# Late sums one at a time in the projection, and GpSimd as the starter of half the block writes

## The reference

```python
shift, scale, gate = jnp.split(jax.nn.silu(c) @ w_ada[layer] + b_ada[layer], 3, axis=-1)
h = rmsnorm(x, norm_g[layer]) * (1.0 + scale[:, None]) + shift[:, None]
u = h @ w_in[layer]
# ... gated delta heads and RWKV heads from u ...
x = x + gate[:, None] * (jnp.concatenate([ya, yb], axis=-1) @ w_out[layer])
```

## Time and profile before

| | |
|---|---|
| profiled execution | 3534.95 us, span 3533.2 us |
| granted TensorE clock, mean | 0.924 |
| projection | 0 to about 1468 us; TensorE busy 1191.83, VectorE 834.79 |
| product L2018, one per pair period | first at 309.4, last at 876.2 us: 81.0 us apart |
| recurrence, 1468 to 2070 | TensorE busy 504.81, VectorE 301.16, ScalarE 136.51, GpSimd 0.13 |
| L2049, sums of 128 x 512 | 240, 180.4 us busy; 239.4 us of standing ahead of them |
| L1365, starts of reads by GpSimd | 256, 137.5 us |

### The profile page before, as it was taken

How to read it: one execution, slowest core, us unless ns; L and a number is a source line. 1 busy time by engine, 2 the same in 40 slices (tenths; PEclk the granted TensorE clock), 3 DMA queues, 4 the chain that set the end, 5 groups by cost and what they waited for, 6 DMA issues and landing times. The chain is left out here.

```text
span 3533.2 us, 71437 instructions
## 1 busy us (share of the span) xinstructions
PE 2973.7 (84%) x30614; PEld 2473.7 (70%) x30614; DVE 2012.3 (57%) x3463; ACT 1012.2 (29%) x1636; POOL 708.9 (20%) x526
## 2 busy tenths in 40 slices
PE   5898888878788888388998967886979999998897
PEld 2586777666667777388888856775867877786484
DVE  5556556565554565345555556774241799997123
ACT  3243334333232222112222223322012444323102
POOL 0001111110010111000000000002864334374283
PEclk9899999988888998699999979997999999999998
DMA  9525555545555556323333224433423222221322
GB/s 388 199 76 156 154 171 166 163 152 162 171 179 175 189 180 202 118 81 94 96 86 101 74 83 145 130 115 152 155 84 125 79 83 78 84 84 60 119 95 72
DMA packets 265242, 465.90 MB, mean 132 GB/s; under 512 B 108224, under 2 KB 156576, under 8 KB 258544
## 3 DMA queue, kind: packets, MB, share of 16 engines
q1 hardware_dynamic: 213152, 364.52, 31.4%
q0 software_dynamic: 20672, 67.27, 6.5%
q10 hardware_dynamic: 31120, 29.72, 2.7%
HBM read 382.40 MB, written 81.63 MB: 131 GB/s over the span
## 5 line engine op out<-in xcount | busy, mean ns | idle before, releaser
L1365 POOL DMA_DIRECT2D arena_p<-in_w_ada x256 | 137.5, 537 | 1208.2 <-DVE arena_p L2049 624.3
L1139 PE MATMUL pjl<-high,w_high 128*128 128x512 f32 x816 | 325.4, 399 | 29.0 <-DVE low L2810 16.4
L1140 PE MATMUL pjl<-low,w_high 128*128 128x512 f32 x816 | 320.8, 393 | 0.0
L1141 PE MATMUL pjl<-high,w_low 128*128 128x512 f32 x816 | 320.6, 393 | 0.0
L2049 DVE SCALAR_TENSOR_TENSOR arena_p<-arena_p,csk 128x512 f32<-128x512 f32 x240 | 180.4, 752 | 239.4 <-DMA arena_p<-in_w_ada 235.0
L3238 DVE SCALAR_TENSOR_TENSOR arena<-arena,par 128x512 f32<-128x512 f32 x232 | 293.1, 1263 | 6.8
L1122 POOL TENSOR_TENSOR w_low<-ring_o,w_high 128x1024 fp32r<-128x1024 f32 x88 | 226.7, 2576 | 6.9
L1249 PE MATMUL xu<-h_high,wh_in 128*128 128x512 f32 x512 | 221.0, 432 | 0.0
L2880 POOL TENSOR_TENSOR w_low<-ring_o,w_high 128x1024 fp32r<-128x1024 f32 x64 | 169.3, 2646 | 250.1 <-ACT w_high L3067 249.7
L1120 POOL TENSOR_TENSOR w_high<-ring_o,cst 128x1024 fp32r<-128x1024 f32 x88 | 171.1, 1944 | 213.0 <-PE pjl L1141 67.8
L1268 DVE TENSOR_TENSOR wl_in<-ring,wh_in 128x1024 fp32r<-128x1024 f32 x136 | 165.9, 1220 | 82.8 <-ACT wh_in L1261 82.5
(11 more groups left out here) (506 smaller groups left out, 6922.4 us busy)
## 6 DMA issues: line engine op xcount, KB each, us to landing
ring<-in_w_lr SPq DMA_DIRECT2D x136, 512.0 KB, 4.5
arena_p<-in_w_ada POOLq DMA_DIRECT2D x256, 256.0 KB, 3.5
arena_p<-in_w_ada SPq DMA_DIRECT2D x32, 1024.0 KB, 8.8
ring_o<-in_w_out SPq DMA_DIRECT2D x64, 512.0 KB, 3.8
ring_o<-in_w SPq DMA_DIRECT2D x64, 512.0 KB, 3.8
arena_r<-rk_d SPq DMA_DIRECT2D x47, 384.0 KB, 4.7
rk_d<-arena_p SPq DMA_DIRECT2D x72, 192.0 KB, 2.0
arena_p<-gate_rows SPq DMA_DIRECT2D x32, 386.0 KB, 6.5
```

The costliest lines, as they stand in the source:

```text
L1139: pe.matmul(lat, wh[:, c], ah, start=kk == 0, stop=False)
L1140: pe.matmul(lat, wh[:, c], al, start=False, stop=False)
L1141: last = pe.matmul(lat, wl[:, c], ah, start=False, stop=kk == KT - 1)
L1365: pool.dma_start(late[:, x % 2], io["w_ada"][8 + x // 16, :, x % 16]).then_inc(S[f"p_la{x % 2}"], 16)
```

## The change

1. `later(n)` becomes `later(due)`: one call does at most one sum, and none once `due` sums are done. The calls are spread over the lines between VectorE's other work, also inside `sums` and `streams`.
2. The 16 sums leave the front and stand beside the LoRA mixes, the gate chain and the first mixes; their four column products move to the start of period 0, into the columns `pair_cols`, and TensorE waits there for `late_kept(0)` (p_ld) before the LoRA products.
3. GpSimd's first 16 reads are cut in two, 11 and 5, with the first two pairs of gate rows between.
4. Three sums of every period but the first are done in the tail of the one before.
5. In the recurrence GpSimd starts the four block writes that ScalarE started, on a semaphore of their own (r_g1); SyncE waits for both.

```diff
@@ front_vector, columns
             parts(2)
-            later(6)
             weights(6)
             row(6)
-            later(6)
             weights(7)
             row(7)
-            later(4)
             mods(3)
@@ gpsimd, projection
-            late_reads(pool, 0, 16)
-            front_pool(pool)
+            late_reads(pool, 0, 11)
+            front_pool(pool, lambda: late_reads(pool, 11, 16))
             late_reads(pool, 16, 256)
@@ tensor, period
+                if i == 0:
+                    pe.wait_ge(S["p_ld"], 1)
                 lora_products(0)
@@ tensor
             columns()
-            late_columns(pe, front_cols, 16)
...
             pe.wait_ge(S["b_gc"], 6)
+            late_columns(pe, pair_cols, 16)
@@ vector, sums and streams
                     link(dve.tensor_tensor_scan(...))
+                later(16 * i + 32)
                 dve.tensor_tensor(sg, cs, sg, ALU.subtract).then_inc(S["p_cs"], 1)
...
                 link(dve.tensor_tensor(bb, kk, av, ALU.mult))
+                later(16 * i + 32)
...
                 dve.tensor_tensor(bb, bb, gn, ALU.mult)
+                later(16 * i + 32)
                 dve.tensor_tensor(kd, kd, gn, ALU.mult)
+                later(16 * i + 32)
                 dve.tensor_tensor(sg, kk, sg, ALU.mult)
@@ vector, head
                 if more:
                     weights(m + 2)
-                    later(3)
+                    later(due)
                     weights(m + 3)
-                    later(3)
+                    later(due)
                 dve.wait_ge(S["q_nl"], 48 * (h + 1))
                 link(dve.tensor_tensor(qkv[:, 1], qkv[:, 1], sqk, ALU.mult))
+                later(due)
                 dve.scalar_tensor_tensor(qkv[:, 0, 0:LAT], ...)
+                later(due)
                 for d in range(2):
                     link(dve.tensor_tensor(KB[:, d], KB[:, d], qkv[:, 1], ALU.mult))
+                    later(due)
                 for d in range(2):
                     dve.tensor_tensor(KBG[:, d], KB[:, d], EG[:, d], ALU.mult)
+                    later(due)
@@ vector, period
                 link(dve.scalar_tensor_tensor(kk, k, prm(i, R_KK), nr, ALU.mult, ALU.mult))
+                later(due)
                 sums(i, 0)
-                later(2)
+                later(due)
                 weights(m + 2)
-                later(1)
+                later(due)
                 weights(m + 3)
-                later(2)
+                later(due)
                 streams(i, 0)
-                later(1)
+                later(due)
...
                 sums(i, 1)
-                later(3)
+                later(due)
                 weights(m + 6)
-                later(3)
+                later(due)
                 streams(i, 1)
+                while x_[0] < due:
+                    later(due)
...
                 if i < PAIRS - 1:
+                    later(due + 1)
                     mixes(i + 1, 2, "p_mv")
+                    later(due + 2)
                     weights(m + 9)
+                    later(due + 3)
@@ vector, later
-            def later(n):
-                for x in range(x_[0], min(x_[0] + n, 256)):
+            def later(due):
+                x = x_[0]
+                if x < due:
@@ gpsimd, recurrence
+            for a in range(2 * PAIRS):
+                pool.wait_ge(S["r_pa"], a * 2 + 2)
+                blocks_out(pool, e, LT[a % 2], range(4, 8), S["r_g1"])
@@ sync, recurrence
-                blocks_in(sp, e, S, "r", a, LBr, LB)
+                blocks_in(sp, e, S, "r", a, LBr, LB, (("r_h1", 64), ("r_g1", 64)))
@@ scalar, recurrence
-                act.wait_ge(S["r_pa"], a * 2 + 2)
-                blocks_out(act, e, S, "r", a, LT[a % 2], range(4, 8))
```

More of the change, by code:

```diff
@@ L408, in front_scalar, with front_vector @@
         return columns, logits, exponential, decays
-    def front_vector(dve, weights, link, later):
+    def front_vector(dve, weights, link):
         def normed(k0, k1):
@@ L570, in front_vector, with front_pool @@
         return columns, softplus, cumulated, products_of, kept
-    def front_pool(pool):
+    def front_pool(pool, reads):
         pool.wait_ge(S["b_scan"], 2)
@@ L580, in front_pool @@
             pool.dma_start(gate_rows[1, d], bt[96 + 8 * d:104 + 8 * d]).then_inc(S["b_out"], 16)
+        reads()
         pool.wait_ge(S["b_eg"], 2)
@@ L681, in hops @@
             sp.wait_ge(S["g_ltc"], 2 * a + 2)
-            blocks_out(sp, e, S, "g", a, LT[a % 2], range(8))
-            blocks_in(sp, e, S, "g", a, LBr, LB)
+            blocks_out(sp, e, LT[a % 2], range(8), S["g_h1"])
+            blocks_in(sp, e, S, "g", a, LBr, LB, (("g_h1", 128),))
             inverse_out(sp, e, S, "g", a, ZBr, ZB)
@@ L701, in delta_sync @@
                 sp.wait_ge(S["g_ltc"], 2 * (m + 2) + 2)
-                blocks_out(sp, e, S, "g", m + 2, LT[m % 2], range(8))
-                blocks_in(sp, e, S, "g", m + 2, LBr, LB)
+                blocks_out(sp, e, LT[m % 2], range(8), S["g_h1"])
+                blocks_in(sp, e, S, "g", m + 2, LBr, LB, (("g_h1", 128),))
             if m + 3 < GH:
@@ L1151, with blocks_out @@
     ("BT", "turn0", "next", "LC", "left1", "CT", "right1", "MB", "turn1", "left2", "MC", "right2", "turn2"))}
-def blocks_out(eng, e, S, q, a, LT, of):
+def blocks_out(eng, e, LT, of, there):
     for g in of:
@@ L1159, in blocks_out, with blocks_in @@
         eng.dma_start(e["lb_d"][:, g].rearrange("u (i j) -> i u j", j=16),
-                      LT[s].rearrange("p d u t -> p (d u) t")[:, :, at:at + 16]).then_inc(S[q + "_h1"], 16)
-def blocks_in(sp, e, S, q, a, LBr, LB):
-    sp.wait_ge(S[q + "_h1"], 128 * a + 128)
+                      LT[s].rearrange("p d u t -> p (d u) t")[:, :, at:at + 16]).then_inc(there, 16)
+def blocks_in(sp, e, S, q, a, LBr, LB, shares):
+    for there, n in shares:
+        sp.wait_ge(S[there], n * (a + 1))
     for d, dst in enumerate((LBr[0:48], LB[64:112])):
@@ L1961, in head @@
                 more = h < GH - 1
+                due = 16 * h + 160 if more else 0
                 if h:
@@ L2061, in late_kept @@
                     dve.tensor_tensor(mod2[:, k], cols, pr("b_ada2", 48)[:, k], ALU.add).then_inc(S["p_ld"], 1)
-            columns, softplus, cumulated, products_of, kept = front_vector(dve, weights, link, later)
+            columns, softplus, cumulated, products_of, kept = front_vector(dve, weights, link)
             def tables():
@@ L2093, in _ @@
             lora_mix(0)
-            late_kept(0)
+            later(16)
             weights(10)
             lora_mix(1)
+            later(16)
             weights(11)
@@ L2099, in _ @@
             lora_mix(2)
+            later(16)
             lora_mix(3)
+            later(16)
             weights(12)
+            later(16)
             cumulated(0)
+            later(16)
             weights(13)
+            later(16)
             mixes(0, 0, None)
+            later(16)
             weights(14)
+            later(16)
             cumulated(1)
+            later(16)
             weights(15)
+            later(16)
             mixes(0, 1, "p_kr")
+            later(16)
             weights(16)
+            later(16)
             mixes(0, 2, "p_mv")
+            later(16)
             products_of()
             weights(17)
+            later(16)
             kept()
+            later(16)
+            assert x_[0] == 16
             for i in range(PAIRS):
```

19 lines of the change are left out of this document (10 added, 9 removed).

## The result

| | median us | range, runs |
|---|---|---|
| before, on the same chip | 3538.8 | 3533.5 to 3558.7, 4 |
| changed kernel | 3408.0 | 3400.9 to 3424.8, 4 |

The ratio is 0.963, 95% interval 0.957 to 0.968: faster, by 131 us. The profiled execution took 3401.2 us (span 3399.2), 134 less than that of before. Forecast were 78 less, 3457 us in a range of 3420 to 3510. The direction was right and the time is outside the range.

The account below looks back on a forecast made before the run. A chain through VectorE, whose late sums stand 235.0 us for reads, was taken to bound the projection. Pairs -53 and -4, heads -9, front -9, recurrence -3 gave -78: 3457 us, range 3420 to 3510.

Parts of the forecast that it names:

- The last tile follows as before.: Pair periods: TensorE's last tile, behind the bonus product, was taken to keep its length, a change of 0.
- a rival at 0.12: More gain than forecast: TensorE keeps full clock in the pairs, seven times 2 to 3 us, L at 3.5: 3425 us; chance 0.12.
- With L = 4.2 this part is 1.0 us later.: Pair period, reciprocal to end of streams(0): three sums each add L + 0.75, a change of 3L - 11.6 us.
- L: Time from the end of sum x-2 to when sum x can start; taken as 4.2 us in pairs, 3.5 in heads.
- The two rows near 5 us: Pair period: two profiled sums with L of 5.1 and 5.4 us; 4.2 was taken as nearer the median landing.
- The second sum now follows the second split and ends at about 1156.4.: Heads, ahead of the stores: start of a count giving 3L - 8.6 us per head, with L = 3.5.
- Now two sums and a split, 2.6: -3.2.: Heads, convolution end to product L1931: 5.8 us falls to 2.6, a gain of 3.2 us per head.
- of the second about 1.9 remain: Front: TensorE's second gap, 5.65 us at 163.29, shrinks to about 1.9, a gain of 3.7 us.
- near 73: Pair periods: the period of 81.0 us was to fall to near 73, otherwise the forecast counts as wrong.
- the 57 of the sum: Pair periods' whole forecast gain: -53 us for seven periods and -4 for the first.
- The recurrence's -3: Recurrence, GpSimd starting ScalarE's four block writes: -4 us from the negated copy's waits, +1 from later block reads.
- The lock-out: VectorE's two-port mode blocks GpSimd's descriptor writes, 2.5 us on every read, +35 us in all; chance 0.02.

Follow-up runs that it names:

- the two fillers: Kernel before, with 40 or 56 matmuls nobody reads on TensorE ahead of its wait for each pair period's bonus product: ratios 0.9988 and 0.9941.
- the dead products: Changed kernel with three 128x768 products nobody reads on VectorE right before each pair period's bonus product: ratio 0.9728 to the kernel before.
- the blocks and heads runs: Kernel before with one part changed: GpSimd starting ScalarE's block writes in the recurrence (0.9984), or one-by-one sums in the heads only (0.9918).
- The run with three buffers of 344: Changed kernel reading and summing only 344 of 512 columns per late block, in three buffers instead of two: ratio 0.9374 to the kernel before.
- pairs alone: Kernel before with one-by-one sums in the eight pair periods only; front, heads and block writes as before: ratio 0.9762.
- the two spread kernels without filler: Changed kernel with fewer sums ahead of the heads' stores, more in later waits (0.9481); then also two per pair period moved into the store wait (0.9453).

## Why the prediction was wrong, step by step

The main mechanism stood: the sums left the stretch behind sums(1), which gave -73.7 against -71, and GpSimd's four writes cost nothing that can be measured. Four steps failed, each in the direction of too small a gain.

**"The last tile follows as before."** The tail was taken at no change. Shown wrong by the two fillers and the dead products: it is about 3 us shorter when TensorE runs at full clock behind the bonus product, -14.9 here. I had this as a rival at 0.12, with 2 to 3 us seven times, and 3425 us. It belonged into the sum, since I had priced the clock in the front, with the earlier trace rows, and in the pairs not. Three tails stay slow, two of them behind waits of 2.7 and 5.0 us, which is why it isn't -22.

**"With L = 4.2 this part is 1.0 us later."** The formula held: in the period shown L is 3.4 (start at 390.00), 4.9 and 3.4, mean 3.9, and 13.5 + 3 x 3.9 = 25.2 against 25.0 measured. Its size was off: over the eight periods the stretch is 24.6, which is L = 3.7 by the formula, and before it was 25.4 in the mean where my row had 25.1. Forecast +8, measured -6.6, together 14.6 us. Most of the -6.6 can't be told from scatter: in the blocks and heads runs, whose pair periods are as before, the same stretch is 24.7 us. So one by one is level there, not 1 us later. The two rows near 5 us were high picks. Over all sums of the pair periods that waited for a read, L is 3.9 us in the median and 4.2 in the mean before, and 3.8 and 4.2 after. The run with three buffers of 344 shows that the reads do set this stretch.

**"The second sum now follows the second split and ends at about 1156.4."** That is 7.9 us behind L1956's end, and it contains the read wait of 3.87 us of the third sum of a batch, which no longer stands there. It ends 3.7 us behind in six of seven heads. Against that L is 4.1 there by the formula, not 3.5: 4.2 less 1.8 is the 2.4 by which the stretch came out shorter than forecast, 17 us in seven heads. A wait must be taken out with the instruction that waits. With the sums spread out, the same stretch is 15.5 us, so the eight sums were no free move either: the changed kernel gave away 5 us a head.

**"Now two sums and a split, 2.6: -3.2."** Measured -4.7. From the convolution to the product L1931 it was 5.8 us in the row and 6.2 in the mean of the heads, and is 2.4 now; and I left out the second sum ahead of the first SiLU product (two in a batch, now one), another 0.9. Together 10 us.

The front: "of the second about 1.9 remain" was right (1.81), but I let only the first gap's clock loss go. The clock behind the second gap is 1.00 instead of 0.66 too: 3.4 us of the 4 that were missing. Against the period "near 73": it is 68.7 between bonus products (69.5 from reciprocal to reciprocal). "TensorE's wait for L2018 falls from 92.7 to about 35 us": it is 14.5. The stretches from reciprocal to bonus product lost 77.7 us (6.6 and 73.7, less 2.6) instead of the 57 of the sum, and 92.7 less 77.7 is 15; so this is mostly the step on L again, not the tail. The read waits were to "fall by less than half": they fell by 63%. The recurrence's -3 did not come: TensorE's waits for the negated copy went as forecast, and from the last head to the end it is still 0.4 us longer.

The lock-out that the Trainium skill (SBUF — State Buffer, section "SBUF: two separate sides") gives for GpSimd's starts wasn't seen: 256 starts took 538 ns in the median and 742 at most, with one sum between VectorE's products everywhere. Whether these products use the mode that locks GpSimd out, no run shows.

## What to carry to other kernels

- When an edit closes a gap of TensorE, sum the clock behind the gap as well: here 11.6 us of standing cost 3 us more in the tile behind it, and matmuls that nobody reads, 56 per period, won 21 us in a kernel.
- Spread small jobs with a turnaround over the whole period, and look first at where the engine stands still. Two reads in flight at 3.9 us each, and 0.75 us a sum, allow one sum in 2.3 us. Eight of them in the 20 us ahead of the stores held the stores up; with four of the eight elsewhere that stretch is 5 us shorter, though the sums wait no less.
- Before using a row as a size, read it in every period. When the instruction that waits is moved, its wait goes with it.

## What the runs showed that I had not expected

- A short wait of TensorE is not always free of the clock's cost, and its length alone does not tell. In the pair periods of the changed kernel, pairs alone, the runs with 40 matmuls and with dead products, and the two spread kernels without filler, 6 of 17 waits of 1.1 to 1.9 us for the bonus product have a slow tail behind them, and 10 of 11 of 2.2 to 3.3 us. The eleventh, 2.46 us, has a granted clock of 1.00 and a tail of 16.1, and one of 1.30 us has 0.91 and 17.8.
- Reads of 344 instead of 512 columns made the whole kernel 1.5% shorter with two buffers. L fell in the pairs from 3.8 to 3.1 us in the median of the sums that wait.
- Spread out, the reads are no faster: L is 5.0 us in the heads of the spread kernels and 3.5 in the changed one, in the median of the sums that wait. Their waits come to 132.1 us, more than the changed kernel's 87.7, in a kernel that is 1.8% faster: 84.9 us of them lie in the waits for the stores, where VectorE would stand anyway (20.9 in the changed kernel), and ahead of the heads' stores they fell from 34.7 to 11.2.

```profile
DVE arena_p L2079 <- DMA arena_p<-in_w_ada: 132.1, 88, 3.8
PE tp L1555 <- ACT arena_p L1712: 45.5, 8, 21.0
PE tp L1370 <- DVE arena_p L2044: 9.6, 5, 3.0
```

The total of a wait is no measure of what it costs; TensorE's own, 78.5 to 45.5 and 14.5 to 9.6 us up to the last head, are nearer to it.
